# First layer's values multiplied as eight full-width units before all pairs; second layer's first output units split one step earlier

## The reference, cut to what matters

```python
# layer 0: w_in has 3 groups of query columns, then shared K, shared V (1024 columns each), then 4 cross heads
parts = split_cols(h @ even_w_in[j], [ATTN_W] * N_DIL + [ATTN_W, ATTN_W, CROSS_WIDTH])
mix = mixer_dilated(parts[:N_DIL], parts[N_DIL], parts[N_DIL + 1], rel_bias)   # 16 heads of 64
cross = cross_attention(qc, mem_n, w_mem_kv[i])
x = x + jnp.concatenate([mix, cross], axis=-1) @ w_out[i]
```

## Time and profile before

| | us |
|---|---|
| Median of 3 executions (lowest, highest) | 1532.45 (1531.69, 1534.11) |
| The profiled execution, device time | 1534.58 |
| Its span in the trace | 1532.8 |
| TensorE busy in the span | 1513.6 (99%) |
| VectorE busy | 1316.3 (86%) |
| ScalarE busy | 1124.7 (73%) |
| GpSimd busy | 95.3 (6%) |

### The profile page before, as it was taken

How to read it: one execution, slowest core, us unless ns; L and a number is a source line. 1 busy time by engine, 2 the same in 40 slices (tenths; PEclk the granted TensorE clock), 3 DMA queues, 4 the chain that set the end, 5 groups by cost and what they waited for, 6 DMA issues and landing times.

```text
span 1532.8 us, 25011 instructions
## 1 busy us (share of the span) xinstructions
PE 1513.6 (99%) x8132; PEld 1280.9 (84%) x8132; DVE 1316.3 (86%) x1783; ACT 1124.7 (73%) x1487; POOL 95.3 (6%) x70
## 2 busy tenths in 40 slices
PE   9999999999999999999999999999999999999997
PEld 8999978888898788888888888888888888888886
DVE  5788868777778879998998998998998998998997
ACT  6565566544557668788788888788788888878875
POOL 2422100000030000000000000000000000000000
PEclk9999999999999989999999999999999999999999
DMA  9944546666633579999999999999999999999992
GB/s 283 241 138 137 152 129 190 190 186 192 170 90 90 164 291 369 391 380 390 381 369 389 378 374 385 380 377 376 382 396 360 384 395 358 387 391 352 401 385 112
DMA packets 225973, 455.39 MB, mean 297 GB/s; under 512 B 12848, under 2 KB 119488, under 8 KB 225920
## 3 DMA queue, kind: packets, MB, share of 16 engines
q1 hardware_dynamic: 221712, 439.52, 79.5%
q0 software_dynamic: 4208, 15.22, 3.9%
HBM read 445.52 MB, written 9.18 MB: 297 GB/s over the span
## 4 chain that ended last, share of the span: by engine, by line
PE 93%; DVE 4%; ACT 1%; issue 1%; DMA 0%; SPq 0%; ACTq 0%; DVEq 0%
PE ps L815 26%; PE ps L817 26%; PE ps L816 26%; PE ps L1139 5%; PE ps L1141 3%; PE ps L1327 2%; PE ps L931 2%; PE ps L967 1%; PE ps L947 1%; DVE w_lo L1824 1%; PE ps L1269 0%; DMA big<-in_w_mem_kv 0%; DVE X L2030 0%; DVE small L1920 0%; DVE pr L2190 0%
## 5 line engine op out<-in xcount | busy, mean ns | idle before, releaser
L1824 DVE TENSOR_TENSOR w_lo<-big,w_hi 128x1024 fp32r<-128x1024 f32 (+1 forms) x830 | 977.6, 1217 | 121.4 <-ACT w_hi L1711 52.2
L1711 ACT CAST w_hi<-big 128x1024 fp32r<-128x1024 f32 x672 | 693.5, 1056 | 139.1 <-PE ps L817 135.5
L815 PE MATMUL ps<-w_hi,m_hi 128*128 128x512 f32 (+1 forms) x1008 | 392.6, 389 | 1.5 <-DVE w_lo L1824 1.3
L817 PE MATMUL ps<-w_hi,m_lo 128*128 128x512 f32 (+1 forms) x1008 | 389.7, 387 | 0.0
L816 PE MATMUL ps<-w_lo,m_hi 128*128 128x512 f32 (+1 forms) x1008 | 389.6, 386 | 0.0
L815 PEld LDWEIGHTS ps<-w_hi,m_hi 128*128 128x128 f32 x1008 | 189.5, 188 | 41.5 <-issue 4.3
L817 PEld LDWEIGHTS ps<-w_hi,m_lo 128*128 128x128 f32 x1008 | 189.5, 188 | 38.2
L816 PEld LDWEIGHTS ps<-w_lo,m_hi 128*128 128x128 f32 x1008 | 189.6, 188 | 36.9
L1364 ACT CAST w_hi<-big 128x1024 fp32r<-128x1024 f32 (+2 forms) x166 | 164.8, 1003 | 39.5 <-PE ps L817 32.4
L815 PE MATMUL ps<-w_hi,h_two 128*128 128x512 f32 (+1 forms) x464 | 182.1, 392 | 0.0
L817 PE MATMUL ps<-w_hi,h_two 128*128 128x512 f32 (+1 forms) x464 | 179.5, 387 | 0.0
(11 more groups left out here) (309 smaller groups left out, 1560.6 us busy)
## 6 DMA issues: line engine op xcount, KB each, us to landing
big<-in_odd_w_gate SPq DMA_DIRECT2D x112, 1024.0 KB, 7.3
big<-in_odd_w_up SPq DMA_DIRECT2D x112, 1024.0 KB, 7.7
big<-in_odd_w_down SPq DMA_DIRECT2D x112, 1024.0 KB, 7.6
big<-in_even_w_in SPq DMA_DIRECT2D x42, 512.0 KB, 4.3
big<-in_even_w_gate SPq DMA_DIRECT2D x22, 512.0 KB, 4.6
big<-in_even_w_up SPq DMA_DIRECT2D x22, 512.0 KB, 3.9
big<-in_even_w_down SPq DMA_DIRECT2D x22, 512.0 KB, 4.7
big<-in_w_out SPq DMA_DIRECT2D x20, 512.0 KB, 3.7
```

The source lines that it names most:

```text
L815: mm(dst, a[0], b[0], start=start, stop=False, **kw)
L817: return mm(dst, a[1], b[0], start=False, stop=stop, **kw)
L1711: nc.scalar.copy(w_hi[:, slot, :], ring[s][:, (u % 2) * UNIT:(u % 2 + 1) * UNIT]).then_inc(s_hi, 1)
L1824: return V.tensor_tensor(dst, src, lead.bitcast(F32), ALU.subtract)
```

## The change

Layer 0's values are no longer a unit of each pair. Their weight, 1024 rows by 1024 columns, is loaded as eight units of whole rows (unit c: rows 128c to 128c+127, all 1024 columns). `values_unit(c)` multiplies the tokens by it, with the tokens as the stationary side: 12 matmuls of 512 columns, adding up over c in four PSUM banks. The result has tokens on the partitions already, so nothing is turned. ScalarE copies the four banks to `XH` (`values_out`), which is free at that time, and `mix` reads a pair's 128 columns of it. All eight units run before pair 0. A pair then has four units (`mats`), and the third branch's scores always lie in bank 4, so p(1) and not p(0) waits for them to be read.

The steps are written in another order: TensorE's is p(0, 1, 2), turn head 0, p(3), turn head 1, `scores(nxt)`, `mix(now)`. VectorE no longer scales head 1's probabilities in the first eight pairs; ScalarE does (`second_probs`). ScalarE's `exps` of head 1 stands ahead of `e(1)`. In pair 7's step output unit 1 is multiplied ahead of head 1's turn, and pair 8's step has one unit less. TensorE's steps are all written out, with no loop. `OUT_MADE` of layer 1 has its first unit in step 4 instead of 5, and one unit more or less in the later steps.

```diff
-OUT_MADE = {5: (0,), 6: (1, 2), 7: (3, 4), 8: (5, 6, 7), 9: (8, 9)}
+OUT_MADE = {4: (0,), 5: (1,), 6: (2, 3), 7: (4, 5), 8: (6, 7), 9: (8, 9)}
...
+        for c in range(DC):
+            add(("values", c), (c + 2) % SLOTS)
         for g in range(PAIRS):
-            for m in range(NBR + 2):
+            for m in range(NBR + 1):
...
+        def value_bank(t, hf):
+            return ps[:, ((3, 4), (2, 7))[t][hf], :]
...
-                if m == 0 and norm is None:
-                    pe.wait_ge(S["third_read"], PAIRS if pair.cross else pair.g)
+                if pair.cross:
+                    pe.wait_ge(S["third_read"], PAIRS)
+                elif m == 1 and pair.g > 0:
+                    pe.wait_ge(S["third_read"], pair.g)
...
+            def values_unit(c):
+                w = split(0, 0, [U.at[("values", c)]], 1)
+                pe.wait_ge(s_nlo, DC * NORM_MIX0 + c + 1)
                 for t in range(TT):
-                    last = tr(value_bank(pair)[:, tok(t)], vT[:, tok(t)], ident)
-                last.then_inc(S["turned_v"], 1)
+                    if c == 0:
+                        pe.wait_ge(s_me, 2 * t + 2)
+                    for hf in range(2):
+                        last = mm3(value_bank(t, hf), part(HS, A_, c, tok(t)), part(w, A_, 0, slice(hf * 512, (hf + 1) * 512)),
+                                   c == 0, c == DC - 1, skip_group_check=True)
...
-                    v = vN[:, :, :]
+                    v = XH[:, :, pair.g * P:(pair.g + 1) * P]
...
-                    ahead = {LATE: ((), (0,)), LATE + 1: ((1, 2), (3,)), LATE + 2: ((4, 5), (6,))}[now.g]
+                    ahead = {LATE: ((0,), (1,)), LATE + 1: ((2,), (3,)), LATE + 2: ((4, 5), (6,))}[now.g]
...
-                p(0)
-                turn_values(now)
-                p(1)
+                p(0, 1, 2)
                 turn_probs(now, 0)
-                p(2, 3)
+                p(3)
                 turn_probs(now, 1)
                 scores(nxt)
-                p(4)
                 mix(now)
...
+            def second_probs(pair):
+                S = s_at[0]
+                act.wait_ge(S["summed"], 2 * pair.g + 2)
+                act.wait_ge(S["dve_rden"], 2 * pair.g + 2)
+                for t, (a, b) in enumerate(((0, P), (P, CAUSAL))):
+                    last = A(probs(pair, 1)[:, a:b], tmp[:, a:b], ACT.Copy, scale=rden[:, 1, t:t + 1])
+                last.then_inc(S["probs"], 1)
...
                     e(0)
-                    values()
                     h(0)
+                    exps(now, 1)
                     e(1)
-                    exps(now, 1)
                     h(1)
+                    e(2)
                     probsT(now, 0)
-                    e(2)
+                    second_probs(now)
                     h(2)
                     e(3)
+                    h(3)
                     probsT(now, 1)
-                    h(3)
-                    e(4)
                     h(4)
```

More of the change, by code:

```diff
@@ L620, in stream_loads @@
                 span = range(1, PAIRS // 2)
+                for c in range(DC):
+                    load(0, 0, [U.at[("values", c)]], w_in[0][:, c:c + 1, (NBR + 1) * D:(NBR + 2) * D])
                 load_pair(pair_at(0, 0))
@@ L1035, in stream @@
                 first = pair_at(0, 0)
+                for c in range(DC):
+                    values_unit(c)
                 for m in range(first.mats):
-                    project(first, m, norm if m == 0 else None)
-                pe.wait_ge(s_me, 2 * 2)
+                    if m < 2:
+                        pe.wait_ge(s_vout, m + 1)
+                    project(first, m)
+                pe.wait_ge(s_vout, 2 * TT)
                 scores(first)
-                steps(pe, step)
+                for g in range(NPAIR):
+                    step(pair_at(0, g), *(pair_at(0, h) if h < NPAIR else None for h in (g + 1, g + 2)))
                 for ch in range(LATE, NPAIR):
@@ L1419, in evac @@
                     act.wait_ge(S["mixed"], 2 * pair.g - 1)
[L1420 to L1422 removed]
+                dst = qT[:, pair.par, m, :] if m < pair.nbr else kT[:, pair.par, :]
                 nc.scalar.copy(dst, ps[:, pair.bank(m), 0:SEQ]).then_inc(S["evacuated"], 1)
@@ L1473, in e @@
                         evac((nxt, aft)[m], 0)
-                def values():
-                    if not now.cross:
-                        act.wait_ge(S["turned_v"], now.g + 1)
-                        nc.scalar.copy(vN[:, :, :].rearrange("p t n -> p (t n)"), value_bank(now)).then_inc(S["values"], 1)
                 exps(now, 0)
@@ L1544, in step_odd, with values_out, stream @@
                     mix_hi(g)
-            def stream(done):
+            def values_out(t, hf):
+                if (t, hf) != (1, 1):
+                    act.wait_ge(s_vmade, 2 * t + hf + 1)
+                else:
+                    act.wait_ge(s_used, U.at[("values", DC - 1)] + 1)
+                nc.scalar.copy(XH[:, t, hf * 512:(hf + 1) * 512], value_bank(t, hf)).then_inc(s_vout, 1)
+            def stream():
                 act.sem_inc(s_at[0]["probsT"], 1)
                 a, b = pair_at(0, 0), pair_at(0, 1)
-                for m in range(done, a.mats):
+                for c in range(2, DC):
+                    hi(0, 0, [U.at[("values", c)]])
+                for m in range(3):
                     hi_mat(a, m)
+                for t in range(TT):
+                    for hf in range(2):
+                        values_out(t, hf)
+                hi_mat(a, 3)
                 for m in range(a.mats):
@@ L1580, in _ @@
                 hi(0, 0, [U.at[("mem", n)]])
-            for m in range(3):
-                hi_mat(pair_at(0, 0), m)
+            for c in range(2):
+                hi(0, 0, [U.at[("values", c)]])
             mem_out(1)
             act.wait_ge(s_scrw, 16)
-            stream(3)
+            stream()
             def half_copy(i, first, ns):
@@ L1941, in head_probs @@
                     dve.wait_ge(S["probs_turned"], n + 1)
+                if pair.kind == "even" and hh:
+                    return
                 for t, (a, b) in enumerate(((0, n0), (n0, n0 + SEQ))):
@@ L1955, in step @@
                     low(0)
-                    if isinstance(now.g, int) and now.g == LATE:
-                        head_probs(now, 1)
-                        low(1)
-                    else:
-                        low(1)
-                        head_probs(now, 1)
+                    head_probs(now, 1)
+                    low(1)
                     low(2)
```

46 lines of the change are left out of this document (19 added, 27 removed).

## The result

The changed kernel takes 1539.16 us (median of 12 runs, 1536.65 to 1543.29), the kernel before 1533.30 beside it (12 runs, 1531.37 to 1534.25). The ratio is 1.004 with a 95% interval of 1.003 to 1.005: slower by 0.4%, where 1531.3 was forecast and the range ended at 1535.6. The profiled execution took 1537.85 us with a span of 1536.0, against 1534.58 and 1532.8.

A forecast was written before the change was run, and what follows sets the result against it. TensorE was taken to bound the kernel (93% of the chain). First layer −1.0 us (1.5 gained, 0.5 given back at pair 7) and layer 1 −0.2 make −1.2: from 1532.45 to 1531.3 us, range 1528.0 to 1535.6.

The forecast's parts named there:

- The stage of the values and pair 0: First layer's start: eight value units take 21.8 us, a gain of 1.2; pair 0's scores come at 71.9.
- 14.7 + 1.3: First step, pair 0's to pair 1's scores: 14.7 us of TensorE work plus 1.3 of waits, bounds 0 and 2.
- The start: Rival, chance 0.04: the first value unit's load comes late and TensorE stands 2 to 4 us at 37.96, giving 1534.
- The ordinary step: First layer, six steps from pair 1's to pair 7's scores: 15.51 us each on TensorE, 93.1 together.
- is not the limit: Ordinary step: VectorE loses a split (1.22 us) and a scaling, so it does not bound the step.
- The rival that I had put beside it (ScalarE): Rival, chance 0.17: ScalarE bounds the step, the keys' copy having 0 to 0.4 us to spare; +5 us, 1536.3.
- the sign that I had named: First layer's steps: forecast wrong if steps exceed 15.6 us, with the wait for `kT` over 0.2 in each.
- Pair 7: First layer: new 3.8 us wait ahead of output unit 0; scores to output unit 4 take 30.3 against 29.81, giving back 0.5.
- a rival at 0.07: Clock rival, chance 0.07: TensorE's clock falls behind pair 7's new wait, costing 2.5 us and more, giving 1534.
- The second layer: `w_lo` waits of 1.3 us go, wait at pair 6's second turn grows 1.1; net −0.2, bounds −1.3 and +1.1.

The follow-up runs named there:

- a1: Changed kernel with GpSimd's mask sums released by VectorE's first reads of the next scores instead of head 1's probabilities: 1534.78 us, ratio 1.0005.
- c2: Changed kernel with GpSimd's three mask sums of a pair in one instruction, released at the same place: 1544.26 us, one run.
- c1: Changed kernel with 14 matmuls whose result nobody reads in pair 7's wait, ahead of output unit 0: 1536.52 us, ratio 1.0019.
- d2: Changed kernel with unused matmuls in pair 7's wait and in the second layer's waits ahead of pair 6's turns: 1535.39 us, ratio 1.0020.
- a3: Changed kernel with the second layer's splits of output units back where they were (OUT_MADE of before): 1539.12 us, ratio 1.0035.
- c4: Changed kernel with masks released later and pair 9's copy ahead of head 1's Exps in pair 7, second layer as changed: 1529.53 us, ratio 0.9973.
- a2: Changed kernel with ScalarE's copy of pair 9's projection ahead of head 1's Exps in pair 7's step, as before: 1533.37 us, ratio 0.9997.
- d3: Changed kernel with nothing altered, profiled a third time: 1541.88 us.
- d1: Changed kernel with nothing altered, profiled a second time: 1539.04 us.

## Why the prediction was wrong

**The stage of the values and pair 0: right.** The value units last from 37.49 to 59.34, 21.85 us (21.8 summed). Pair 0's scores start at 71.52, pair 1's 16.03 us later (14.7 + 1.3 = 16.0). The size of the waits was right, their place was not: I had spread them over the two turns and the copy of the keys, and there is one, of 0.84 us, ahead of p(3) for `qT`. The start didn't starve.

**The ordinary step: wrong, and the largest miss.** Its sum on TensorE holds (15.51 against 15.54 in a1). What failed is the sentence that VectorE loses a split and a scaling "and is not the limit". I priced its splits at 1.22 us each, from a row of the kernel before, and didn't look at what GpSimd does in the same time. Here it is, in the trace of the kernel before, around pair 2's scores (107.20); VectorE first, then GpSimd's sums:

```profile
106.34 1.22 DVE L1824 TENSOR_TENSOR w_lo<-big,w_hi 128x1024 fp32r<-128x1024 f32 x1
108.53 1.25 DVE L1824 TENSOR_TENSOR w_lo<-big,w_hi 128x1024 fp32r<-128x1024 f32 x1 [0.97 <-ACT w_hi L1364]
```

```profile
106.62 2.08 POOL L756 TENSOR_TENSOR big<-big,con 128x512 f32<-128x512 f32 x1 [13.37 <-DVE pr L1943]
...
108.65 2.28 POOL L756 TENSOR_TENSOR big<-big,con 128x512 f32<-128x512 f32 x1
```

GpSimd starts behind a split that VectorE has begun, and VectorE's next one comes after a pause. So GpSimd waits, twice, and nobody wants its sums soon. The change shortens the step but not ScalarE's and VectorE's part in it. GpSimd's release, the probabilities of head 1, now comes at S − 1.2, ahead of two splits in a row, and VectorE waits twice: from 103.35 to 103.80, and from 104.9 to 106.0. Each time it is for the rest of a GpSimd instruction. That is 1.4 us (3.79 less two splits), of which 0.4 is absorbed ahead of the scores' end. The remaining 1.0 passes down the chain, from the scores' reading over head 0's sum and the Exps of head 1 to the copy that p(3) waits for. There TensorE had 0.4 in hand (in a1 the copy ends at S + 11.52 and p(3) starts at S + 11.96), and the step is 16.17 us instead of 15.54 (a1) or 15.51 (the sum): 3.8 to 4.0 us in six steps. The bracket's 0.37 is less than this, because it counts only from the modelled end of the turn before. The rival that I had put beside it (ScalarE) had a slack of the right size, but the wrong engine, and the wrong copy, that of the keys, for which TensorE doesn't wait in any of these steps. That it came nearest with 1536.3 is luck. And the sign that I had named, a wait for `kT` over 0.2, didn't appear; only the step's length, over 15.6, gave the miss away. The Trainium skill (SBUF — State Buffer, "Who interferes with whom") states the rule: a VectorE instruction with two inputs in SBUF and a GpSimd instruction that reads SBUF shut each other out, for a whole instruction, and whichever starts first goes first. The trace agrees, with 1.22 us against 1.58 and 2.29 for the same split, and in c2 with 3.75, up to the end of GpSimd's one long instruction. It is the rule that I should have weighed.

**Pair 7: the wait right, its consequence not.** Output unit 0 starts 12.77 us behind the scores (12.8 summed), after a wait of 3.54 us (3.8 summed). The stretch to output unit 4 is 31.8 us instead of 30.3. The missing 1.5 is the clock (1.57 in c1), which I had as a rival at 0.07, because a wait of 1.25 us had not moved it. But I had written myself that no row of before has a wait of 3.8 us; with no row to decide it, one in fourteen was far too little.

**The second layer: the waits right, the clock again not.** The waits for `w_lo`, 1.3 us before, are gone, and the waits ahead of pair 6's turns grow by 1.3 (1.1 summed), though at the first turn and not, as I had it, at the second. But the 1.26 and 0.60 us together bring the clock down, and 1.6 us go (d2). Instead of −0.2 the stretch costs +1.1.

**Between the profiled and the median execution.** In the two first profiles the stretch from the routing to the end went 2.07 us in favour of the changed kernel. Without it and the 0.47 at the start, the three stretches that the change reaches give 2.59 + 2.02 + 1.13 = 5.7 us, and the medians lie 5.9 apart. That these agree so well is in part luck: a3 and c4 give no sign of the second layer's 1.1 us in the medians (their intervals are wider than it), and the lower clock at 10 to 15 us, seen only in profiles of changed kernels, is not in the sum. What the experiments show is the first layer's part: 3.8 us in the steps (a1), 1.6 by the clock at pair 7 (c1) and 3.1 by the wait there (a2), the last of which was in the forecast.

**What the change was worth.** It takes 3.3 us off each step of TensorE (18.84 to 15.54) and adds 21.8 at the start; that this leaves a gain was right. Two places in other engines' programs, GpSimd's release and the place of one copy, decide whether it is seen: 1529.5 us (c4) or 1539.2.

## What to carry to other kernels

When a step gets shorter on the bounding engine, the others' work moves against each other: read what every engine does beside the operations whose price you take from a row, GpSimd too, and ask whether both read SBUF. Where a helper engine's work is released by a semaphore that merely happens to be late enough, release it where the other engine reads PSUM. A new wait of TensorE, longer than those that your rows show with the clock unmoved, is to be priced with the clock behind it; if it can't be removed, try matmuls without a use in it, which were worth 1.6 us here each time.

## What the runs showed of the hardware

The exclusion between VectorE and GpSimd was new to me in its sizes. The same 128x1024 split took 1.22, 1.58, 2.29 or 3.75 us, depending on how much of a GpSimd instruction was still ahead of it, and GpSimd's 128x512 sum took 1.28 or 2.08 to 2.29. Beside VectorE's readings from PSUM and its reductions it took 1.30 (a1), and neither lengthened.

TensorE's granted clock stayed at 1.00 through single waits of 1.25 us and 0.84, and fell behind one of 3.54 and behind the pair 1.26 and 0.60. The waits' length alone doesn't decide it: at 8 to 12 us it stayed at 1.00 behind waits of 0.70 and 1.22 us (the kernel before) and fell behind 0.49 and 1.29 (d3). Each fall behind the two new waits cost 1.6 us, and none came when the same wait was filled with matmuls (c1, d2).

In the routing the clock differed between two executions of one kernel, which moved its time by up to 2.8 us (976.6 in d1, 979.5 in d3). Of such a program's time, a difference under 3 us between two single profiles says nothing until it is taken apart by stretches.
